# A hybrid decoder step on one Trainium2 core: a third slot of split weights for the memory's keys and values, low parts moved to VectorE, and a new order of the norms between them

## What is computed

```python
h = rms_norm(x, g_mix_pre); proj = h @ w_in
y_a, S1, shift1 = rwkv_branch(...)       # recurrence, then a group norm over each head
y_b, buf1 = conformer_branch(...)        # convolution, layer norm, silu, @ w_pw
mixed = (g_a * y_a + g_b * y_b) @ w_out; x = x + rms_norm(mixed, g_mix_post)
hm = rms_norm(mem, g_mem); mem_k = hm @ w_k; mem_v = hm @ w_v     # 256 memory tokens
x = x + rms_norm(attention(x @ w_q, mem_k, mem_v) @ w_o_x, g_x_post)
x = x + rms_norm((silu(gt) * up) @ w_down, g_ffn_post)
S_t = S_{t-1} diag(w_t) + (S_{t-1} a_t) b_t^T + v_t k_t^T         # also once for each sample
```

## Time and profile before

| | us |
|---|---|
| median of 3 runs | 1208.33 (1208.24 to 1209.09) |
| the profiled execution's own time | 1207.61 |
| its span in the trace | 1205.9 |
| TensorE busy | 1143.2 (95% of the span) |
| stretch from the first key block to the end of the mix | 431.8 to 573.3 |

### The profile page before, as it was taken

How to read it: one execution, slowest core, us unless ns; L and a number is a source line. 1 busy time by engine, 2 the same in 40 slices (tenths; PEclk the granted TensorE clock), 3 DMA queues, 4 the chain that set the end, 5 groups by cost and what they waited for, 6 DMA issues and landing times.

```text
span 1205.9 us, 25556 instructions
## 1 busy us (share of the span) xinstructions
PE 1143.2 (95%) x10914; PEld 1078.0 (89%) x10914; DVE 569.2 (47%) x987; ACT 435.9 (36%) x732; POOL 382.6 (32%) x192
## 2 busy tenths in 40 slices
PE   7999999999999987689899989999999999999994
PEld 7999899998999986479899957999999999999993
DVE  4567777667766445925546194362322223200005
ACT  4543432432423456322645343562232222222212
POOL 4331211220311233544622300332344433344442
PEclk9999999999999998899899999999999999999996
DMA  7321111120112422264614677321333323223311
GB/s 200 88 71 37 36 54 37 54 67 22 54 54 63 123 72 88 61 212 128 176 44 150 193 246 278 100 85 36 95 95 89 87 87 103 84 81 96 96 30 71
DMA packets 163465, 115.90 MB, mean 96 GB/s; under 512 B 5272, under 2 KB 153002, under 8 KB 163113
## 3 DMA queue, kind: packets, MB, share of 16 engines
q1 hardware_dynamic: 159835, 104.87, 29.1%
q10 hardware_dynamic: 3542, 9.75, 2.5%
HBM read 108.91 MB, written 6.17 MB: 95 GB/s over the span
## 4 chain that ended last, share of the span: by engine, by line
PE 46%; issue 35%; POOL 9%; DVE 6%; ACT 2%; DMA 1%; POOLq 0%; SPq 0%; DVEq 0%; ACTq 0%
PE ps L424 34%; PE ps L406 9%; POOL w_lo L734 9%; PE ps L845 2%; DVE cache L2472 1%; DVE sq_acc L2371 1%; DMA q_bc<-q_scratch 1%; DVE ps L2383 1%; DMA x_tok<-in_x_prompt_dram 0%; DVE x_res L2387 0%; DVE h_lo L2404 0%; DVE ps L2400 0%; DVE stat L2445 0%; ACT h_hi L1778 0%; DVE h_lo L2461 0%
## 5 line engine op out<-in xcount | busy, mean ns | idle before, releaser
L734 POOL TENSOR_TENSOR w_lo<-w_raw,w_hi 128x1024 fp32r<-128x1024 f32 (+1 forms) x141 | 327.4, 2323 | 646.1 <-ACT w_hi L459 646.1
L424 PE MATMUL ps<-h_hi,w_hi 128*128 128x260 f32 x1376 | 289.8, 292 | 8.1 <-DVE h_lo L2336 4.7
L424 PE MATMUL ps<-h_hi,w_lo 128*128 128x260 f32 x1376 | 277.9, 284 | 0.0
L424 PE MATMUL ps<-h_lo,w_hi 128*128 128x260 f32 x1376 | 277.5, 283 | 0.0
L424 PEld LDWEIGHTS ps<-h_hi,w_hi 128*128 128x128 f32 x1376 | 213.1, 189 | 19.4 <-POOL w_lo L734 7.9
L459 ACT ACTIVATE w_hi<-w_raw 128x1024 fp32r<-128x1024 f32 (+2 forms) x142 | 140.9, 993 | 207.1 <-PE ps L424 182.7
L424 PEld LDWEIGHTS ps<-h_hi,w_lo 128*128 128x128 f32 x1376 | 212.9, 189 | 0.0
L424 PEld LDWEIGHTS ps<-h_lo,w_hi 128*128 128x128 f32 x1376 | 212.6, 189 | 0.0
L2079 DVE SCALAR_TENSOR_TENSOR conv_y<-glu,prm,conv_y 128x512 f32<-128x512 f32 x120 | 102.6, 855 | 2.2
L845 PE MATMUL ps<-g,axb 64*64 64x128 f32 (+1 forms) x1024 | 78.0, 254 | 2.1 <-DVE g L2105 2.1
L2581 DVE TENSOR_TENSOR f_tmp<-ps,silu 128x520 f32<-128x520 f32 x19 | 13.3, 700 | 137.6 <-PE ps L424 137.6
(11 more groups left out here) (399 smaller groups left out, 2028.4 us busy)
## 6 DMA issues: line engine op xcount, KB each, us to landing
w_raw<-in_w_gate_up_dram SPq DMA_DIRECT2D x44, 512.0 KB, 3.9
w_raw<-in_w_in_dram SPq DMA_DIRECT2D x38, 512.0 KB, 4.0
cache<-in_cache_mem_k_dram SPq DMA_DIRECT2D x16, 512.0 KB, 6.6
cache<-in_cache_mem_v_dram SPq DMA_DIRECT2D x16, 512.0 KB, 6.1
w_raw<-in_w_down_dram SPq DMA_DIRECT2D x16, 512.0 KB, 4.0
w_raw<-in_w_k_dram SPq DMA_DIRECT2D x8, 512.0 KB, 4.0
w_raw<-in_w_v_dram SPq DMA_DIRECT2D x8, 512.0 KB, 3.7
w_raw<-in_w_out_dram SPq DMA_DIRECT2D x8, 512.0 KB, 3.9
```

The costliest lines, as they stand in the source:

```text
L424: mm = nc.tensor.matmul(ps[:, 2 * s + a, 0:width], w[:, k, :], x[:, x0 + k, a * width:(a + 1) * width], start=(first and k == 0 and n == 0 ...
L734: pool.tensor_tensor(lo[:, 0:kts], w_raw[:, b % RAW_SLOTS, 0:kts], hi[:, 0:kts].bitcast(F32), ALU.subtract).then_inc(w_lo_ready, 1)
```

## The change

A third pair of slots for `w_hi`/`w_lo` in blocks 39 to 53 (`sx_hi`, `sx_lo`), and a slot of its own for block 38 (`kx_hi`, `kx_lo`). Both lie in memory whose earlier contents are done with by then: the squares of the memory tokens, half of `kt`, and the samples' window. A block may now be split when block b-3 is multiplied. The low parts of blocks 41 to 53 (13 blocks) are made on VectorE in place of GpSimd, which makes 38, 39 and 40 and then waits for 53. The steps of the norms stand one at a time between blocks of keys and of values. The samples' state update is divided: two steps before the mix, and one after each of the first three pairs of mix blocks; its store moves to the tenth mix block, and the wait for the store from ahead of the `x_tok2` load to ahead of block 72. The loops of the mix on ScalarE and VectorE are written out. ScalarE's Silu and high parts of the convolution move behind the group norms' roots, the copy of the first half of the values stands between them, and TensorE no longer waits for the copy of the values before it turns the keys back.

```diff
+    cursor[0] = k_base
+    sx_hi = buf("sx_hi", [P, KT, P], F32R)
+    sx_lo = buf("sx_lo", [P, KT, P], F32R)
+    cursor[0] = pair_base + 4 * KT * NT + 4 * KT // 2 * MEM
+    kx_hi = buf("kx_hi", [P, KT, P], F32R)
+    cursor[0] = attn_base + 2 * 4 * KT * MEM
+    kx_lo = buf("kx_lo", [P, KT, P], F32R)
...
+        if b == B_K:
+            return kx_hi[:, :], kx_lo[:, :]
+        if B_K < b < B_MIX:
+            n = (b - B_K - 1) % 3
+            return (sx_hi[:, :], sx_lo[:, :]) if n == 2 else (w_hi[:, n], w_lo[:, n])
...
+        if b in (B_K, B_K + 3):
+            return None
+        if B_K < b < B_MIX + 2:
+            return b - 2
...
-            split_lows(2, B_MIX)
+            split_lows(2, B_K)
+            pool.wait_ge(conv_ready, 1)
+            for b in range(B_K, B_K + 3):
+                split_lo(b)
+            pool.wait_ge(w_lo_ready, B_MIX)
             split_lows(B_MIX, B_OUT)
...
-            key_block(2)
-            conv_var(2)
-            conv_var(3)
-            key_block(3)
             pe.wait_ge(ln_centred, NP)
             pe.wait_ge(y_landed, 16)
             for p in range(NP):
                 mm = tr(ps[:, 4, B * p:B * p + B], y_rows[:, P * p:P * p + P], ident[0:B, 0:B])
             mm.then_inc(y_turned, 1)
+            key_block(2)
+            conv_var(2)
+            conv_var(3)
+            key_block(3)
+            gn_mean(0)
             key_block(4)
-            gn_mean(0)
             gn_mean(1)
             key_block(5)
             gn_var(0)
             gn_var(1)
             key_block(6)
             gn_mean(2)
+            key_block(7)
             gn_mean(3)
-            key_block(7)
+            dense_values(pe, 0, 0)
             gn_var(2)
+            dense_values(pe, 0, 1)
             gn_var(3)
-            for a in range(2):
-                for u in range(4):
-                    dense_values(pe, a, u)
-            pe.wait_ge(out_taken[1], B_MIX // 2)
-            pe.wait_ge(out_taken[0], B_MIX // 2)
+            dense_values(pe, 0, 2)
+            dense_values(pe, 0, 3)
+            for u in range(4):
+                dense_values(pe, 1, u)
...
+            split_lo(B_K + 3)
+            dve.wait_ge(y_turned, 1)
+            V.tensor_copy(y_fm[:, :, T:NT], ps[:, 4, 0:NP * B].rearrange("p (c b) -> p c b", b=B)).then_inc(y_ready, 1)
+            split_lo(B_K + 4)
+            split_lo(B_K + 5)
+            conv_scale(0)
+            conv_scale(1)
             gn_centre(0)
+            conv_scale(2)
+            conv_scale(3)
+            split_lo(B_K + 6)
             gn_centre(1)
+            split_lo(B_K + 7)
+            split_lo(B_V)
             gn_scale(0)
             gn_scale(1)
+            split_lo(B_V + 1)
             gn_centre(2)
+            split_lo(B_V + 2)
             gn_centre(3)
+            split_lo(B_V + 3)
             gn_scale(2)
+            split_lo(B_V + 4)
             gn_scale(3)
-            for j in range(NP):
-                dve.wait_ge(rwkv_hi, j + 1)
-                tt(h_lo[:, NP + j], y_fm[:, j], h_hi[:, NP + j].bitcast(F32), ALU.subtract).then_inc(rwkv_lo, 1)
-            link_v(tt(ss[:, :, :], ss[:, :, :], over_i(vs[:, 4, :]), ALU.mult))
-            link_v(tt(ss_tmp[:, :, :], over_j(vs_sa[:, :]), over_i(vs[:, 3, :]), ALU.mult))
-            link_v(tt(ss[:, :, :], ss[:, :, :], ss_tmp[:, :, :], ALU.add))
-            link_v(tt(ss_tmp[:, :, :], over_j(vs_v[:, :]), over_i(vs[:, 1, :]), ALU.mult))
-            tt(ss[:, :, :], ss[:, :, :], ss_tmp[:, :, :], ALU.add).then_inc(ss_made, 1)
...
+            split_lo(B_V + 5)
+            conv_low(0)
+            conv_low(1)
+            split_lo(B_V + 6)
+            conv_low(2)
+            conv_low(3)
+            rwkv_low(0)
+            split_lo(B_V + 7)
+            rwkv_low(1)
+            rwkv_low(2)
+            rwkv_low(3)
+            sample_state(0)
+            sample_state(1)
...
+                gated(m)
+                if m < 3:
+                    sample_state(2 + m)
```

More of the change, by code:

```diff
@@ L437, in dense_values @@
         b = B_V + 4 * a + u
+        hi, lo = weights(b)
         pe.wait_ge(w_lo_ready, b + 1)
@@ L1678, in gn_root, with value_out @@
                 go(ln_buf(j), ln_buf(j), ACT.Exp, scale=-0.5).then_inc(gn_rsqrt, 1)
-            key_out(4)
+            def value_out(a):
+                act.wait_ge(block_done, B_V + 4 * a + 4)
+                go(v_tok[:, :, 512 * a:512 * (a + 1)], ps[:, 2 * a:2 * a + 2, :], ACT.Copy).then_inc(out_taken[a], 4)
+            log_exp_table()
+            conv_square(0)
+            conv_square(1)
+            key_out(0)
+            act.wait_ge(n_mem.lo, n_mem.split + KT)
+            split_hi(B_K + 3)
+            key_out(1)
+            split_hi(B_K + 4)
+            conv_square(2)
+            conv_square(3)
+            key_out(2)
+            split_hi(B_K + 5)
+            act.wait_ge(ln_var, NP)
+            link_a(go(two(rs[:, :]), ps[:, 6:8, 0:HALF], ACT.Ln, bias=eps[:, 2:3]))
+            go(rs[:, :], rs[:, :], ACT.Exp, scale=-0.5).then_inc(ln_rsqrt, 1)
+            key_out(3)
             split_hi(B_K + 6)
             gn_square(0)
+            key_out(4)
+            split_hi(B_K + 7)
             gn_square(1)
             key_out(5)
-            split_hi(B_K + 7)
+            split_hi(B_V)
             gn_root(0)
@@ new lines, in _, with gated @@
+            split_lo(B_V + 5)
[11 more added lines that the diff above has]
+            sample_state(1)
+            def gated(m):
+                taken = B_MIX // 2 + m + 1
+                ga, gb = two(gate_a[:, m]), two(gate_b[:, m])
+                dve.wait_ge(block_done, B_MIX + 2 * m + 1)
+                stt(gb, out_view(0), prm_col("b_pw", m), gb, ALU.add, ALU.mult).then_inc(out_taken[0], 1)
+                dve.wait_ge(block_done, B_MIX + 2 * m + 2)
+                tt(ga, out_view(1), ga, ALU.mult).then_inc(out_taken[1], 1)
+                dve.wait_ge(out_taken[0], taken)
+                dve.wait_ge(out_taken[1], taken)
+                tt(gb, ga, gb, ALU.add).then_inc(merged, 1)
@@ L2331, in _ @@
+            for m in range(KT):
+                gated(m)
+                if m < 3:
+                    sample_state(2 + m)
             dve.wait_ge(merged, KT)
```

143 lines of the change are left out of this document (70 added, 73 removed).

## The result

| | before | changed |
|---|---|---|
| median | 1208.28 (1207.78 to 1209.09, 4 runs) | 1175.11 (1173.82 to 1177.39, 4 runs) |
| ratio | | 0.9727, 95% interval 0.9710 to 0.9744 |
| profiled execution, its span | 1207.61, 1205.9 | 1173.82, 1172.1 |
| first key block to the last mix block's end | 431.8 to 573.3: 141.5 | 431.9 to 541.2: 109.3 |

All times are in us. The forecast was 1175.6 with a range of 1170.5 to 1187. The kernel is 33 us faster, and 32.2 of the 33.8 that the span lost lie in the stretch that the change rewrites. That the median comes within 0.5 us of the forecast is in part luck: four runs of the changed kernel alone lie 3.6 us apart. The firmer test of the forecast is the stretch.

The account below looks back on a forecast made before the run. PE, busy 95% of the span, was taken as the bound. Of 35.2 us not work, less 1.2 and 1.6 of new waits, 32.4 would be won; with the walk's 33, the forecast was 1175.6 us, range 1170.5 to 1187.

Parts of the forecast that it names:

- The sum from the work: First key block to mix end: 106.3 us of PE work in 141.5, so 35.2 at most to win.
- The walk: Four engines' lists stepped through in the new order with the rows' durations and 0.06 us hops; mix ends 33 us earlier.
- The waits: PE's waits among keys and values: none from key 1 to value 5; the 5.2 us one gone.
- The term of 1.2: Last value blocks, behind the convolution's branch: new PE waits of 1.0 us at value 6 and 0.2 at value 7.
- The granted clock: PE's clock from 436 us on: stays at 1.00, where four falls had cost 7.9 us.
- Low parts on VectorE: Thirteen key and value blocks: 1.22 us each, adding 15.9 us to VectorE and taking thirteen times 2.3 off POOL.
- State update in the mix: First mix blocks: state steps and POOL's low parts delay each other, low part late by 0.8 twice, 1.6 us.
- Key 0 unchanged: First key block: stays at 4.4 us, paced by the memory's own low parts, which the change leaves alone.
- Transfers: Moved `x_tok2` load and state store in the mix: given 0, at most 2 us, and 0 to 1 us.
- The pile-up: Rival: new waits on ScalarE's and VectorE's lists interlock, values stay at 4.4 us; 1180 to 1192 us, chance 0.18.
- Late loads: Rival: weight loads arrive late, so the third slot stands empty; 1195 us, chance 0.04.
- A fall of the clock in the stretch, once or throughout: Rivals: two falls, 1180 us, inside the forecast's 0.73; or lower clock from 436 to 492 us, 1231, slower chance 0.02.

Follow-up runs that it names:

- v_values: Changed kernel with the splits of value blocks 6 and 7 ahead of the third and fourth Silu and the first values' copy later: 1173.00 us, ratio 0.9705.
- wait_4steps: Changed kernel with four extra unused VectorE steps of 2.3 us ahead of one key's low part: 1181.20 us, ratio 0.9774.
- state_whole: Changed kernel with all five steps of the samples' state update ahead of the mix's first gate: 1183.61 us, ratio 0.9794.
- v_state: Changed kernel with the last three state steps halved between the gates of six mix pairs and the state's store later: 1177.60 us, ratio 0.9741.
- third_slot_old_order: Kernel before with only the third slot and block 38's own slot added; norms, low parts and state update as before: 1207.67 us, ratio 0.9988.
- v_low39: Changed kernel with block 39's low part also made on VectorE, behind the memory's norm: 1174.62 us, ratio 0.9722.
- order_alone: Changed kernel with the third slot's condition and the VectorE low parts both undone, new order and divided state update kept: 1187.44 us, ratio 0.9827.
- two_slots: Changed kernel with splits of blocks 41 to 55 again waiting for block b-2 in place of b-3: 1187.72 us, ratio 0.9828.

## Why the prediction was right, step by step

**The sum from the work** held. It gave 106.3 us of work in the stretch, 1.2 of new waits in the values and 1.6 in the mix: 109.1; the trace has 109.3. The walk put the first mix block near 492; PE was ready for it at 492.75 (the row of its first matmul starts at 493.17 behind a wait of 0.42). From 431.9 on there were 59.6 of work (106.3 less the mix's 46.7) and 1.2 of waits ahead, which is 492.7. So the mechanism held with the number: the waits and the lower clock went, and what was left was PE's own work.

**The waits.** The 5.2 us for the samples' rows is gone: their copy stands at 441.78, where the walk had 441.9.

```profile
441.78 0.18 DVE L2370 COPY y_fm<-ps 128x32 f32<-128x32 f32 x1
```

At tile 3, with a margin of 0.5, PE did not wait. At value 6 the wait is 0.6, not 1.0. The term of 1.2 was too large in what PE waited; that v_values won 2.0 there shows that a late low part costs more than its wait.

**The granted clock** stayed at the upper level, as forecast. wait_4steps and state_whole show what would have lowered it: it fell after waits of 2.9 and 6.2. The prediction's price for one fall, 2 to 3 us, was a little high: its own four rows give 1.3 to 2.7, and wait_4steps 1.7. Outside the stretch there is a fall in the attention, see below.

**Low parts on VectorE** take 1.22, as the one row of before said. That they take load off POOL was true and of little worth with the new order, 2.1 us.

**State update in the mix.** The mechanism was right, the parts of the size were not. Low parts came late three times by 0.4, 1.2 us in all, where the walk had twice 0.8; the first of the three, at the first mix block, it did not have. From 492.75, when PE was ready, to 541.25 the mix took 48.5 us. 46.7 of work and 1.2 of waits are 47.9, and the other 0.6 is in slow starts behind the waits, which the sum did not have at all. That 1.6 comes near the 1.8 that is measured is luck. POOL's low parts took 2.31, 1.58 and 2.03 us beside the three steps, where "2 to 3.5" was forecast. state_whole and v_state show the mechanism, turns by whole instructions.

The statement that the bank is always in time held, though the weight loads' row of waits names `gate_b`. VectorE's `gate_b` and PE's matmul behind it:

```profile
504.41 0.76 DVE L2411 SCALAR_TENSOR_TENSOR gate_b<-ps,prm,gate_b 128x520 f32<-128x520 f32 x1
```

```profile
505.66 0.50 PE L442 MATMUL ps<-h_hi,w_hi 128*128 128x260 f32 x2 [0.37 <-POOL w_lo L753]
```

The bank was free at 504.41 + 0.76 = 505.17. PE was ready for the block at 505.66 - 0.37 = 505.29 (its weight load 0.2 us earlier), and the low part came last, at 503.22 + 2.31 = 505.53. The other place is alike: bank 517.19, low part 517.66, matmul 517.79. What PE waited for was the low part both times. The expectation of v_state counted these waits once more as "late banks", 1.1 us that were never there to win.

**Key 0 unchanged** was right for this change, and it hid 1.1 us that another edit finds: the memory's low part stands behind POOL's low part for 2.42 us in both kernels.

**Transfers.** One split (at 509.00) waited 2.98 us for its weights, and PE waited nothing for it, as before the change.

**The rest.** From the start of the last `gate_a` (573.45 before) to the end of the span it took 632.5 us before and 630.9 after. This 1.6 us was not in the sum. It isn't the change's: third_slot_old_order, with the old order, has 631.1, and v_low39 and v_state, with the new one, have 632.5 as before did. Over the 14 traces it lies between 630.7 and 632.5. The three long ones differ from the others in the attention, 150 to 160 us behind the last `gate_a`. Here are before and third_slot_old_order, whose orders are alike:

```profile
724.26:734.26 10.00, 8.04 (x53) 7.68 (x52) 9.50 (x37) 3.81 (x6) 0.00 (x0) 0.83 0.97 377
```

```profile
725.71:735.71 10.00, 8.29 (x66) 7.71 (x65) 9.65 (x37) 4.23 (x7) 0.00 (x0) 1.00 0.99 386
```

One has the lower clock there for a while and 53 matmuls in 10 us, the other 66; 8.04 x 0.17 = 1.4 us. v_low39 has the row of the first (8.04, x53, 0.83). The changed kernel has a fall as well, but 15 us earlier:

```profile
681.25:686.25 5.00, 3.77 (x9) 1.68 (x8) 4.16 (x15) 2.21 (x4) 0.00 (x0) 0.66 0.48 193
```

order_alone, two_slots and state_whole fell at that place too, and their 630.7 to 631.3 is no longer than that of the seven traces that fell at neither place. PE has short waits for ScalarE and VectorE around the early place (1.1, 1.2 and 0.9 us), and they seem to take up the slower matmuls: in the 20 us from the early place on (140 to 160 us behind the last `gate_a`) the changed kernel has 90 matmuls and third_slot_old_order, with no fall, 92, where before has 77. So 1.6 us of the 33.8 came from where in the attention the clock fell: at the later place it cost that, at the earlier one nothing. What sets the place is open: the waits ahead of the early place are the same 1.1 and 1.2 us in all 14 traces.

**The rivals.** The pile-up is out: 4.6 us of added work on VectorE cost at most 1.1. Late loads did not come. A fall of the clock in the stretch, once or throughout, did not come either: with PE's waits at 0.4 to 0.6 the granted clock was 1.00 from 436 to 540 us.

## What to carry to other kernels

Where several engines work through lists in a fixed order, first ask what stands ahead of the instruction that fills a slot; a further buffer gave 1.0 us in the old order and 10.2 in the new one, so such parts have to be tried together. Sum the work between two fixed points at the rate of the undisturbed rows and take it from the measured stretch: that difference (35.2 us here) is what an edit can win, and it was the firmest number of this forecast. When VectorE and GpSimd are released by the same event, halving VectorE's steps can make it worse, as every half meets GpSimd again. The starts suggest to place the long steps off that beat instead; no run here tried it.
